# Router columns as weights in four column groups, and the block table built by one-hot products

## Chip, cores and metric

The kernel runs on one core of one Trainium2 chip. The metric is the device time of one execution in microseconds (us). The kernel before takes 2423.96 us, the median of three runs (2423.73 to 2424.24).

## What is computed

One layer of a hybrid backbone over 2048 latent tokens and 256 context tokens of width 1024. Two parallel mixers (an SSD scan with 8 heads, a gated linear attention with 4 heads, both in both directions) share one input and one output projection; then a mixture of experts follows, top 2 of 32 experts, each of inner width 512.

```python
x = x + m_lat[2] * mix_lat
h2_lat = modulate(rmsnorm(x, norm2_g[l]), m_lat[3], m_lat[4])
ffn = moe(h2_lat.reshape(-1, D_MODEL), w_router, router_bias, w_gate[l], w_up[l], w_down[l])
x = x + m_lat[5] * ffn.reshape(x.shape)
...
s = jax.nn.sigmoid((t @ w_router).astype(jnp.float32))          # route(): 2048 x 32 logits
...
dest = pstart[e_sorted] + jnp.arange(T * TOP_K) - start[e_sorted]  # moe(): slot of each choice
buf = jnp.zeros((n_blocks * MOE_BLOCK, D), t.dtype).at[dest].set(t[tok])
yb = lax.map(expert_block, (buf.reshape(n_blocks, MOE_BLOCK, D), block_e))
```

Each of the 4096 choices (2048 tokens, 2 each) gets a slot; a block is 128 slots of one expert. An expert's block needs for each slot the number of its token and its gate. That is the block table.

## The kernel before

It is a row of stages, each a block of per-engine programs that ends with a barrier of all engines: `constants` and `modulation`, `projection`, `chunks`, `mixer`, `slots`, `experts`, `combine`. Within a stage each engine runs its list in the written order, and semaphores tie them.

**mixer** (16 tiles of 128 tokens, 18 steps). In step n, `now` is tile n, `before` tile n-1, `done` tile n-2. TensorE's order in a step is `attn(now)`, `ssd(now)`, `turned_m(before)` (8 transposes), `gla(now)`, `turned_x(done)` (8 transposes), `project(before)` (48 products of 512 columns), `router(done)`. The router's product of a tile is 8 matmuls over the width (L1556): the tile's features `xsT` are the weights, and 32 columns of `w_rt` stream through; the sum stands in 32 columns of the PSUM tile `po`. `gla(now)` waits for `both_done` and `mid_done`, which VectorE signals.

VectorE's order after a projection is `residual(before)` (L1755, x1 = product + x), then, after ScalarE's `squares_x` (L1453) and GpSimd's `rstd` (L1386, L1389), `scaled_x(before)` (L1763), `logits(done)` (L1725), and in the next step `masked_attn` (L1733 twice, L1738) and `state_mid` (L1649). So the lists of both engines meet twice in a step: VectorE's `residual` waits for the last product of `project`, and TensorE's `gla` waits for `state_mid`.

**slots** computes the routing in some 80 VectorE instructions in a chain. The slot numbers come at L2000. GpSimd then writes the block table `slot_tok` into DRAM: it was cleared by one DMA (L1906), and 32 indirect DMAs (L1911), 16 tiles by 2 choices, put a record of 16 words (token, gate) at each slot. VectorE meanwhile computes the plan of the blocks (L2008 to L2027: each block's expert, when to load weights).

**experts**: TensorE first spreads the output gate (L2218), VectorE copies it (L2282), ScalarE and VectorE split the first weights into a high and a low part (L2163, L2289). GpSimd loads the table (L2122), copies the tokens of a block (L2118) and gathers their rows (L2120, `fetch`). TensorE transposes them (`turn`, L2229), ScalarE and VectorE split them (`features`, L2168 and L2295), and the products follow (`wide`, L2236). In the lists of ScalarE and VectorE the splits of the first two weight pieces stand ahead of the features of blocks 0 and 1.

## Time and profile before

| what | value |
|---|---|
| median of three runs | 2423.96 us |
| the profiled execution | 2428.52 us |
| its span | 2426.8 us |
| TensorE busy | 2164.6 us, 89% |
| VectorE busy | 1624.7 us, 67% |
| ScalarE busy | 1137.1 us, 47% |
| GpSimd busy | 529.8 us, 22% |
| mean granted TensorE clock | 0.937 |

How to read it: the span runs from the first to the last instruction, the execution's own time is 1.7 us longer. Busy shares are means over stages with different limits, so what an edit is worth has to be read in its own stage. `mixer` lies at about 902 to 1318 us of the span, `slots` at 1321 to 1401, `experts` at 1404 to 2360, `combine` behind it. TensorE is written PE, its weight load PEld, VectorE DVE, ScalarE ACT, GpSimd POOL.

### The profile page before, as it was taken

To read this page: it belongs to the slowest core of one execution; us is meant where nothing else is said; L and a number is where in the kernel's file an instruction comes from. 1 tells how busy PE (TensorE), PEld (TensorE's weight loads), DVE (VectorE), ACT (ScalarE), POOL (GpSimd) and SP (SyncE) were. 2 spreads that over 40 slices of the span, in tenths; PEclk is the share of its full clock that TensorE was granted. 3 is DMA by queue.
4 is the path that set the end of the run, shared out by engine and by line. 5 is a ranking of instruction groups with operands and counts; after the bars stand their busy time and mean duration, and the time that the engine had idled before them with its cause. 6 is when DMAs were issued, how large, how long until landed. Compare 5 with 4: busy or idle time off the path is not lost. (4 is left out here: it accounts for less than half of the span.)

```text
span 2426.8 us, 36201 instructions
## 1 busy us (share of the span) xinstructions
PE 2164.6 (89%) x11697; PEld 1709.4 (70%) x11697; DVE 1624.7 (67%) x2071; ACT 1137.1 (47%) x1469; POOL 529.8 (22%) x536
## 2 busy tenths in 40 slices
PE   4999999998999987999996059999999999999980
PEld 2777777776777766888885048878788778778760
DVE  1333333433666667777773449999999999999983
ACT  0222222222555533333331047777777777777763
POOL 1000000000000001233322423333332333333332
PEclk7999999999999996899997579999999999999995
DMA  8123334322688745899874426478988779989957
GB/s 317 66 78 108 110 117 145 128 99 85 228 291 295 277 171 191 305 311 293 291 240 113 176 54 207 115 241 275 303 253 274 233 233 356 310 293 309 374 182 293
DMA packets 204877, 530.22 MB, mean 218 GB/s; under 512 B 14929, under 2 KB 46156, under 8 KB 198252
## 3 DMA queue, kind: packets, MB, share of 16 engines
q1 hardware_dynamic: 174904, 424.71, 48.8%
q0 software_dynamic: 26224, 91.57, 15.0%
q10 hardware_dynamic: 3651, 12.65, 1.4%
q8 instruction: 61, 1.00, 0.2%
q14 instruction: 37, 0.30, 0.0%
HBM read 398.64 MB, written 130.24 MB: 218 GB/s over the span
## 5 line engine op out<-in xcount | busy, mean ns | idle before, releaser
L2163 ACT ACTIVATE w_hi_e<-w_gates 128x2048 fp32r (+1 forms) x103 | 197.7, 1920 | 237.1 <-issue 104.1
L2289 DVE TENSOR_TENSOR w_lo_e<-w_gates,w_hi_e 128x2048 fp32r<-128x2048 f32 x103 | 236.4, 2296 | 33.2 <-ACT w_hi_e L2163 33.2
L2289 DVE TENSOR_TENSOR w_lo_e<-w_ups,w_hi_e 128x2048 fp32r<-128x2048 f32 x102 | 233.5, 2289 | 37.0 <-ACT w_hi_e L2163 37.0
L2289 DVE TENSOR_TENSOR w_lo_e<-w_downs,w_hi_e 128x2048 fp32r<-128x2048 f32 x100 | 228.4, 2284 | 0.0
L2163 ACT ACTIVATE w_hi_e<-w_ups 128x2048 fp32r (+1 forms) x102 | 195.2, 1914 | 24.8 <-PE pd_e L2236 22.4
L2163 ACT ACTIVATE w_hi_e<-w_downs 128x2048 fp32r x100 | 191.1, 1911 | 1.0
L614 PE MATMUL pf<-raws,w_in_sb 128*128 128x256 f32 x800 | 177.5, 385 | 1.1 <-DVE raws L695 1.1
L2236 PE MATMUL pg_e<-w_hi_e,x_hi_e 128*128 128x512 f32 x408 | 167.7, 411 | 7.2 <-DVE w_lo_e L2289 7.2
L614 PEld LDWEIGHTS pf<-raws,w_in_sb 128*128 128x128 f32 x800 | 154.1, 193 | 23.0 <-DVE raws L695 1.5
L2141 POOL DMA_INDIRECT x_mid<-yb_e,to_e x50 | 126.9, 2538 | 190.7 <-DVE yb_e L2333 188.6
L2236 PE MATMUL pg_e<-w_lo_e,x_hi_e 128*128 128x512 f32 x408 | 162.1, 397 | 0.0
L2236 PE MATMUL pd_e<-w_hi_e,h_hi_e 128*128 128x512 f32 x400 | 162.1, 405 | 0.0
L2236 PE MATMUL pg_e<-w_hi_e,x_lo_e 128*128 128x512 f32 x408 | 161.9, 397 | 0.0
L2236 PE MATMUL pd_e<-w_hi_e,h_lo_e 128*128 128x512 f32 x400 | 157.9, 395 | 0.0
L2236 PE MATMUL pu_e<-w_hi_e,x_hi_e 128*128 128x512 f32 x400 | 157.9, 395 | 0.0
L2236 PE MATMUL pu_e<-w_hi_e,x_lo_e 128*128 128x512 f32 x400 | 157.9, 395 | 0.0
L2236 PE MATMUL pu_e<-w_lo_e,x_hi_e 128*128 128x512 f32 x400 | 157.9, 395 | 0.0
L2236 PE MATMUL pd_e<-w_lo_e,h_hi_e 128*128 128x512 f32 x400 | 157.9, 395 | 0.0
L614 PE MATMUL pf<-hT,w_in_sb 128*128 128x256 f32 x640 | 143.8, 388 | 0.0
L2118 POOL COPY idx_e<-toks_e 128x1 int32 (+1 forms) x54 | 51.5, 954 | 400.7 <-DMA x_mid<-yb_e,to_e 335.9
L614 PEld LDWEIGHTS pf<-hT,w_in_sb 128*128 128x128 f32 x640 | 124.7, 195 | 17.7
L716 DVE TENSOR_SCALAR fm<-u_raw,cols 128x256 f32<-128x256 f32 x54 | 18.2, 411 | 176.2 <-ACT u_raw L506 176.2
(420 smaller groups left out, 4708.4 us busy)
## 6 DMA issues: line engine op xcount, KB each, us to landing
w_gates<-in_w_gate_dram SPq DMA_DIRECT2D x32, 2048.0 KB, 12.1
w_ups<-in_w_up_dram SPq DMA_DIRECT2D x32, 2048.0 KB
w_downs<-in_w_down_dram SPq DMA_DIRECT2D x32, 2048.0 KB
w_mod_half<-in_w_mod_dram SPq DMA_DIRECT2D x16, 1024.0 KB, 7.0
abc_m<-a_rows SPq DMA_DIRECT2D x16, 1024.0 KB, 4.9
recs<-tok_rec SPq DMA_DIRECT2D x15, 968.0 KB, 7.8
qk_rec<-qk SPq DMA_DIRECT2D x14, 1024.0 KB, 3.9
qk<-qk_rec SPq DMA_DIRECT2D x14, 1024.0 KB
```

What stands on the lines that cost most here:

```text
L614: mm = pe.matmul(pf[n % 2][:, f, :], w[:, k, c0:c0 + P], h[:, k, :], start=(k == 0), stop=(k == KT - 1))
L716: i = dve.tensor_scalar(a, b, wt, cols[:, R_CB + f:R_CB + f + 1], ALU.mult, ALU.add)
L2118: pool.tensor_copy(idx[u][:, :], toks[:, bass.ds(b, 1), 0]).then_inc(idx_ready, 1)
L2141: pool.indirect_dma_start(out=x_mid, out_offset=bass.IndirectOffsetOnAxis(ap=to[u][:, 0:1], axis=0), in_=yb[:, :], in_offset=None, compute ...
L2163: act.activation(w_hi[:, s % 3:s % 3 + 1, :], raw(part, half, place), ACT.Copy).then_inc(hi_done, 1)
L2236: mm = pe.matmul(acc[:, :], a[:, k, :], w[:, s % 3, c], start=start and n == 0, stop=stop and n == 2)
L2289: dve.tensor_tensor(w_lo[:, s % 3:s % 3 + 1, :], raw(part, half, place), w_hi[:, s % 3:s % 3 + 1, :].bitcast(F32), ALU.subtract).then_inc( ...
```

## The change

**In the mixer** the router's product is turned round. The 32 columns of `w_rt` are now the weights and the 128 tokens of `xsT` stream; the matmul of part k goes to column group k % 4 and so to PSUM partitions 32j to 32j+31, so that four sums over two parts each stand under one another. ScalarE copies them (`quartered`), and one step later TensorE adds the four (`logit_sums`, one matmul with the copy as weights and `sum4`, four identities under one another). `logits` on VectorE moves behind `masked_attn` of the next step.

**In slots** the table no longer goes through DRAM. A slot is split into its place in the block and its block. For each of four chunks (choice by half of the tiles) VectorE builds one-hot rows of the place (128 wide) and of the block (68 wide), the latter times the token number and the gate; TensorE multiplies them, 32 matmuls that sum into one PSUM tile, and VectorE copies it to `toks`, which `experts` now reads from SBUF. The clearing DMA, the 32 indirect DMAs and the loading DMA are gone.

```diff
+        sum4, quarters = K["st"][0][:, 0, 0:NE], K["rec"][0][:, D + SW:D + SW + P]
...
             def turned_x(t):
                 if t:
-                    act.wait_ge(log_ps, t)
+                    act.wait_ge(quarter_ps, t)
...
+            def quartered(t):
+                act.wait_ge(quarter_ps, t + 1)
+                if t:
+                    act.wait_ge(log_ps, t)
+                act.activation(quarters[:, :], po[:, 0, 256:256 + P], ACT.Copy).then_inc(quarter_done, 1)
...
+                if done is not None:
+                    quartered(done)
                 if before is not None:
                     squares_x(before)
...
                 for k in range(KT):
-                    mm = pe.matmul(po[:, 0, 256:256 + NE], xsT[:, k, :], w_rt[:, k, :], start=(k == 0), stop=(k == KT - 1))
-                mm.then_inc(log_ps, 1)
+                    j = k % 4
+                    mm = pe.matmul(po[32 * j:32 * j + 32, 0, 256:256 + P], w_rt[:, k, :], xsT[:, k, :], start=(k < 4), stop=(k >= 4))
+                mm.then_inc(quarter_ps, 1)
+
+            def logit_sums(t):
+                pe.wait_ge(quarter_done, t + 1)
+                pe.wait_ge(sum4_done, 1)
+                pe.matmul(po[:, 0, 256 + P:256 + P + NE], quarters[:, :], sum4[:, :], start=True, stop=True).then_inc(log_ps, 1)
...
                     attn(now)
+                if n >= 3:
+                    logit_sums(n - 3)
+                if now is not None:
                     ssd(now)
...
                     router(done)
+            logit_sums(LT - 1)
...
+            dve.tensor_reduce(sum4[:, :], ident[:, :].rearrange("p (j c) -> p c j", j=4), AX, ALU.add).then_inc(sum4_done, 1)
...
                     masked_attn(now)
+                if n >= 3:
+                    logits(n - 3)
+                if now is not None:
                     state_mid(now + CT, now)
...
-                if done is not None:
-                    logits(done)
+            logits(LT - 1)
...
+            for c in range(4):
+                pe.wait_ge(parts_done, c + 1)
+                for i in range(LT // 2):
+                    mm = pe.matmul(table[:, :, :].rearrange("p a b -> p (a b)"), in_place[c % 2][:, i, :],
+                                   parts[c % 2][:, i, :, :].rearrange("p a b -> p (a b)"), start=(c + i == 0), stop=(c == 3 and i == LT // 2 - 1))
+                mm.then_inc(parts_used, 1)
...
-            pool.dma_start(slot_tok.rearrange("(b p) c -> p b c", p=P), zero_i[:, :].rearrange("p (b c) -> p b c", c=16)).then_inc(cleared, 16)
-            pool.wait_ge(cleared, 16)
-            pool.wait_ge(slot_done, 1)
-            for t in range(LT):
-                for j in range(2):
-                    pool.indirect_dma_start(out=slot_tok, out_offset=bass.IndirectOffsetOnAxis(ap=route["slot"][:, t, j:j + 1], axis=0),
-                                            in_=slot_rec[:, t, j, :], in_offset=None).then_inc(scattered, 16)
-            pool.wait_ge(scattered, 16 * 2 * LT)
...
-            then(dve.tensor_copy(slot_rec[:, :, :, 1].bitcast(F32), route["gate"][:, :, :]))
-
...
-            dve.sem_inc(slot_done, 1)
+            then(dve.tensor_scalar(pos_i[:, :, :], route["slot"][:, :, :], P - 1, None, ALU.bitwise_and))
+            then(dve.tensor_copy(pos[:, :, :], pos_i[:, :, :]))
+            then(dve.tensor_tensor(blk_of[:, :, :], slot_f[:, :, :], pos[:, :, :], ALU.subtract))
+            then(dve.tensor_scalar(blk_of[:, :, :], blk_of[:, :, :], 1.0 / P, None, ALU.mult))
+            then(dve.tensor_tensor(val[:, :, :], tok_f[:, :].unsqueeze(2).to_broadcast([P, LT, 2]), pos[:, :, :], ALU.subtract))
+
+            H = LT // 2
+            for c in range(4):
+                j, t, b = c // 2, slice(H * (c % 2), H * (c % 2 + 1)), c % 2
+                if c >= 2:
+                    dve.wait_ge(parts_used, c - 1)
+                dve.tensor_tensor(in_place[b][:, :, :], place[:, :].unsqueeze(1).to_broadcast([P, H, P]),
+                                  pos[:, t, j].unsqueeze(2).to_broadcast([P, H, P]), ALU.is_equal)
+                then(dve.tensor_tensor(in_block[b][:, :, :], bnum[:, :].unsqueeze(1).to_broadcast([P, H, TAB]),
+                                       blk_of[:, t, j].unsqueeze(2).to_broadcast([P, H, TAB]), ALU.is_equal))
+                for n, of in enumerate((val, route["gate"])):
+                    op = dve.tensor_tensor(parts[b][:, :, n, :], in_block[b][:, :, :], of[:, t, j].unsqueeze(2).to_broadcast([P, H, TAB]), ALU.mult)
+                op.then_inc(parts_done, 1)
...
+            dve.wait_ge(parts_used, 4)
+            dve.tensor_tensor(toks[:, :, 0], table[:, 0, :], own[:, :], ALU.add).then_inc(plan_done, 1)
+            dve.tensor_copy(toks[:, :, 1].bitcast(F32), table[:, 1, :]).then_inc(plan_done, 1)
+            dve.wait_ge(plan_done, 2)
...
-            pool.dma_start(toks[:, :, :], slot_tok.rearrange("(b p) c -> p b c", p=P)).then_inc(toks_loaded, 16)
-            pool.wait_ge(toks_loaded, 16)
```

How the lists of the engines change at three places. TensorE in one middle step of the mixer, from the router's product to `gla`, before (lines as in the kernel before):

```order
L1556 MATMUL po_m<-w_rt_m,xsT_m 128x32 x8
L1589 MATMUL at_m<-qk 128x128 x8
L1567 MATMUL py_m<-recs,M_m 128x64 x8
L1575 MATMUL py_m<-st_m,cs_m 128x64 x8
L1575 MATMUL py_m<-st,cs_m 128x64 x8
L1525 MATMUL tr_m<-ident,m_m 128x128 x8
L1607 MATMUL po_m<-recs,both_m 128x128 x2
```

and now (the router's product is L1568, the sum of the quarters L1574, `gla` L1624):

```order
L1568 MATMUL po_m<-xsT_m,w_rt_m 32x128 x8
L1606 MATMUL at_m<-qk 128x128 x8
L1574 MATMUL po_m<-st,recs 128x32
L1584 MATMUL py_m<-recs,M_m 128x64 x8
L1592 MATMUL py_m<-st_m,cs_m 128x64 x8
L1592 MATMUL py_m<-st,cs_m 128x64 x8
L1536 MATMUL tr_m<-ident,m_m 128x128 x8
L1624 MATMUL po_m<-recs,both_m 128x128 x2
```

The eight matmuls of the router give 32 rows of 128 columns instead of 128 rows of 32, and one matmul more stands behind `attn`.

VectorE in the same step, from `residual` to `state_mid`, before:

```order
L1755 TENSOR_TENSOR x_m<-tr_m,x_m 128x512 x2
L1763 SCALAR_TENSOR_TENSOR xs_m<-x_m,rsx_m,scale_bc_m 128x1024
L1725 TENSOR_TENSOR logits<-po_m,rt_shift_m 128x32
L1733 TENSOR_TENSOR am_m<-at_m,incl_bd 128x512 x2
L1738 TENSOR_TENSOR both_m<-am_m 128x512
L1649 SCALAR_TENSOR_TENSOR st_m<-st_m,fc 128x128 x2
```

and now:

```order
L1777 TENSOR_TENSOR x_m<-tr_m,x_m 128x512 x2
L1785 SCALAR_TENSOR_TENSOR xs_m<-x_m,rsx_m,scale_bc_m 128x1024
L1755 TENSOR_TENSOR am_m<-at_m,incl_bd 128x512 x2
L1760 TENSOR_TENSOR both_m<-am_m 128x512
L1747 TENSOR_TENSOR logits<-po_m,rt_shift_m 128x32
L1670 SCALAR_TENSOR_TENSOR st_m<-st_m,fc 128x128 x2
```

`logits` has moved by two places and is still ahead of `state_mid` (L1670 now).

ScalarE at the end of the same step now, where `quartered` is L1441 and `squares_x` L1462 (before, L1453 came straight behind the exponential of `cs_m`):

```order
L1424 ACTIVATE E_m<-E_m 128x512 x2
L1428 ACTIVATE cs_m<-cs_m 128x1024
L1441 ACTIVATE recs<-po_m 128x128
L1462 ACTIVATE recs,ssx_m<-x_m 128x1024
L1513 DMA x_mid<-x_m 128x1024
```

The copy of the quarters stands ahead of `squares_x`.

## Rows read from the trace of the kernel before

**Rows 1.** Stages: span, busy (instructions) of PE, PEld, DVE, ACT, POOL; clock; DMA; GB/s.
```profile
500.00:600.00 100.00, 94.92 (x422) 66.74 (x420) 40.77 (x97) 28.11 (x44) 1.08 (x3) 1.00 0.19 63
...
1020.00:1060.00 40.00, 40.00 (x350) 34.63 (x349) 30.46 (x54) 15.58 (x40) 13.82 (x18) 1.00 0.88 287
...
1320.00:1404.00 84.00, 4.41 (x6) 1.67 (x6) 35.60 (x85) 1.91 (x2) 39.94 (x42) 0.52 0.50 172
...
1600.00:2360.00 760.00, 752.42 (x3450) 605.71 (x3448) 708.21 (x496) 552.14 (x412) 265.75 (x166) 1.00 0.86 283
```
**Rows 2.** Timeline of PE, router to router: start us, duration us, engine, line, instruction, tiles, count.
```profile
1064.45 1.87 PE L1556 MATMUL po_m<-w_rt_m,xsT_m 128*128 128x32 f32 x16
1066.24 1.16 PE L1589 MATMUL at_m<-qk 64*128 64x128 f32 x16
...
1086.70 1.87 PE L1556 MATMUL po_m<-w_rt_m,xsT_m 128*128 128x32 f32 x16
```
**Rows 3.** Timeline of DVE and PEld at the start of `gla`: step 2, then a middle step.
```profile
979.82 0.61 DVE L1649 SCALAR_TENSOR_TENSOR st_m<-st_m,fc 128x128 f32<-128x128 f32 x2
...
980.49 0.93 PEld L1607 LDWEIGHTS po_m<-recs,both_m 128*128 128x128 f32 x4 [1.05 <-DVE both_m L1738]
...
1072.09 0.52 PEld L1607 LDWEIGHTS po_m<-recs,both_m 128*128 128x128 f32 x4
```
**Rows 4.** Timeline of DVE and ACT in that middle step.
```profile
1064.48 1.29 DVE L1755 TENSOR_TENSOR x_m<-tr_m,x_m 128x512 f32<-128x512 f32 x2 [2.33 <-PE tr_m L1545]
...
1065.80 1.06 ACT L1453 ACTIVATE recs<-x_m 128x1024 f32<-128x1024 f32 x1 [6.25 <-DVE x_m L1755]
...
1068.12 1.28 DVE L1763 SCALAR_TENSOR_TENSOR xs_m<-x_m,rsx_m,scale_bc_m 128x1024 f32<-128x1024 f32 x1 [2.35 <-POOL rsx_m L1389]
1069.32 0.18 DVE L1725 TENSOR_TENSOR logits<-po_m,rt_shift_m 128x32 f32<-128x32 f32 x1
1069.42 1.28 DVE L1733 TENSOR_TENSOR am_m<-at_m,incl_bd 128x512 f32<-128x512 f32 x2
...
1071.42 0.61 DVE L1649 SCALAR_TENSOR_TENSOR st_m<-st_m,fc 128x128 f32<-128x128 f32 x2
```
**Rows 5.** Timeline of PEld and PE in the projection: products in column groups of 32.
```profile
90.53 0.16 PEld L267 LDWEIGHTS mod_acc<-w_mod_half,cond_silu 128*32 128x32 f32 x8 [0.33 <-issue]
...
91.42 1.05 PE L628 MATMUL psm<-raws,w_small 128*32 128x256 f32 x16
```
**Rows 6.** Timeline, end of the mixer and `slots`: PE, DVE, ACT and POOL.
```profile
1313.97 3.62 PE L1556 MATMUL po_m<-w_rt_m,xsT_m 128*128 128x32 f32 x16 [0.69 <-ACT xsT_m L1432]
1317.63 0.19 DVE L1725 TENSOR_TENSOR logits<-po_m,rt_shift_m 128x32 f32<-128x32 f32 x1 [6.26 <-PE po_m L1556]
1321.08 1.28 ACT L1877 ACT_TABLE_LOAD   x1 [7.16 <-PEq L107]
...
1355.92 0.18 DVE L2000 CAST slot<-slot_f_r 128x32 int32<-128x32 f32 x1
...
1364.33 0.14 DVE L2027 CAST plan<-eb_r 1x1 int32<-1x1 f32 x1
...
1398.35 0.96 POOL L1911 DMA_INDIRECT slot_tok<-slot_rec_r,slot  x1 [0.30 <-issue]
```
**Rows 7.** Timeline, start of `experts`: PEld, POOL, DVE and PE.
```profile
1404.29 3.49 PEld L2218 LDWEIGHTS pd_e<-ident,mod 128*128 128x128 f32 x16 [53.55 <-issue]
...
1404.83 2.96 POOL L2122 DMA_DIRECT2D toks_e<-slot_tok  x1 [5.52 <-POOLq L107]
...
1411.38 4.49 DVE L2289 TENSOR_TENSOR w_lo_e<-w_gates,w_hi_e 128x2048 fp32r<-128x2048 f32 x2 [1.98 <-ACT w_hi_e L2163]
1414.49 1.43 POOL L2118 COPY idx_e<-toks_e 128x1 int32<-128x1 int32 x1 [6.70 <-DMA toks_e<-slot_tok]
...
1423.83 1.94 PE L2229 MATMUL tx_e<-ident,xg_e 128*128 128x128 f32 x8 [0.65 <-DVE x_lo_e L2295]
...
1425.42 0.78 PE L2236 MATMUL pg_e<-w_hi_e,x_hi_e 128*128 128x512 f32 x1
```

More of the change, by code:

```diff
@@ L198, in build @@
             loaded = [names(f"{n}_loaded") for n in ("gates", "ups", "downs")]
-            slots(nc, A, C, route, slot_tok, weights, loaded, x_mid, h_rows)
-            experts(nc, A, C, route, slot_tok, weights, loaded, h_rows, x_mid)
+            toks = ctx.enter_context(nc.sbuf_tensor("toks", [P, TAB, 2], I32))
+            slots(nc, A, C, route, toks, weights, loaded, x_mid, h_rows)
+            experts(nc, A, C, route, toks, weights, loaded, h_rows, x_mid)
         combine(nc, A, x_mid, out)
@@ L1296, in mixer @@
             sem(n) for n in ("x_added", "x_square", "x_rstd", "x_scaled", "rows_added"))
-        xt_ps, xt_done, log_ps, log_done = (sem(n) for n in ("x_transposed", "xT_done", "logits_product", "logits_done"))
+        xt_ps, xt_done, quarter_ps, quarter_done, log_ps, log_done = (
+            sem(n) for n in ("x_transposed", "xT_done", "logit_quarters", "quarters_copied", "logits_product", "logits_done"))
+        sum4_done = sem("sum_4_done")
         block = ctx.enter_context(nc.Block())
@@ L1724, in logits @@
                 dve.wait_ge(log_ps, t + 1)
-                dve.tensor_tensor(route["logits"][:, t, :], po[:, 0, 256:256 + NE], rt_shift[:, :], ALU.add).then_inc(log_done, 1)
+                dve.tensor_tensor(route["logits"][:, t, :], po[:, 0, 256 + P:256 + P + NE], rt_shift[:, :], ALU.add).then_inc(log_done, 1)
             def masked_attn(t):
@@ L1818, in load_part, with slots @@
                  A[("w_gate", "w_up", "w_down")[n]][0][e].rearrange("(k p) f -> p k f", p=P)).then_inc(w_loaded[n], 16)
-def slots(nc, A, C, route, slot_tok, weights, w_loaded, x_mid, h_rows):
+def slots(nc, A, C, route, toks, weights, w_loaded, x_mid, h_rows):
     logits, plan = route["logits"], route["plan"]
@@ L1852, in slots @@
         last = sb("last", [1, 1])
-        bnum = sb("bnum", [1, TAB])
+        bnum = sb("bnum", [P, TAB])
+        place, own = sb("place", [P, P]), sb("own", [P, TAB])
+        tok_f, val = sb("tok_f", [P, LT]), sb("val", [P, LT, 2])
+        pos_i, pos, blk_of = sb("pos_i", [P, LT, 2], I32), sb("pos", [P, LT, 2]), sb("blk_of", [P, LT, 2])
+        in_place = [sb(f"in_place{b}", [P, LT // 2, P]) for b in range(2)]
+        in_block, parts = [sb(f"in_block{b}", [P, LT // 2, TAB]) for b in range(2)], [sb(f"parts{b}", [P, LT // 2, 2, TAB]) for b in range(2)]
         npf = sb("npf", [1, MAXB // 2])
         slot_f = sb("slot_f", [P, LT, 2])
-        zero_i = sb("zero_i", [P, TAB * 16], I32)
-        slot_rec = sb("slot_rec", [P, LT, 2, 16], I32)
         spare = sb("spare", [P, D])
         excl, tot, pb = ps("excl", [P, LT, NE]), ps("tot", [P, LT, NE]), ps("pb", [P, 512])
-        bias_loaded, made, sig_done, both_done, ranks_ps, lec_done, bend_ps, slot_done, cleared, scattered, chain = (
+        table = ps("table", [P, 2, TAB])
+        bias_loaded, made, sig_done, both_done, ranks_ps, lec_done, bend_ps, parts_done, parts_used, chain = (
             sem(n) for n in ("bias_loaded", "made", "sigmoid_done", "both_done", "ranks_product", "lec_done", "bend_product",
-                             "slots_done", "table_cleared", "scattered", "chain"))
+                             "parts_done", "parts_used", "chain"))
         plan_done, spare_written = sem("plan_done"), sem("spare_written")
@@ L1927, in over_e @@
                 return x.unsqueeze(2).to_broadcast([P, LT, NE])
-            dve.wait_ge(made, 7)
+            dve.wait_ge(made, 8)
             dve.wait_ge(bias_loaded, 16)
@@ L2008, in _ @@
             then(dve.tensor_scalar(last[:, :], bend[0:1, NE - 1:NE], -1.0, None, ALU.add))
-            then(dve.tensor_tensor(blk[:, :], bnum[:, :], last[:, :].to_broadcast([1, TAB]), ALU.min))
+            then(dve.tensor_tensor(blk[:, :], bnum[0:1, :], last[:, :].to_broadcast([1, TAB]), ALU.min))
             then(dve.tensor_tensor(past[:, :, :], by_block(blk[:, :]), by_expert(bend[0:1, :]), ALU.is_ge))
@@ L2027, in _, with experts @@
             then(dve.tensor_copy(plan[:, PL_PAIRS:PL_PAIRS + 1], eb[:, 0:1]))
-            dve.sem_inc(plan_done, 1)
-def experts(nc, A, C, route, slot_tok, parts, w_loaded, h_rows, x_mid):
+            dve.wait_ge(parts_used, 4)
+            dve.tensor_tensor(toks[:, :, 0], table[:, 0, :], own[:, :], ALU.add).then_inc(plan_done, 1)
+            dve.tensor_copy(toks[:, :, 1].bitcast(F32), table[:, 1, :]).then_inc(plan_done, 1)
+            dve.wait_ge(plan_done, 2)
+def experts(nc, A, C, route, toks, parts, w_loaded, h_rows, x_mid):
     mod, ident, plan = C["mod"], C["ident"], route["plan"]
@@ L2130, in _ @@
             pool.wait_ge(gate_done, 2)
-            pool.tensor_copy(to[0][:, :], toks[:, 0, 0:2]).then_inc(to_ready, 1)
+            pool.tensor_copy(to[0][:, :], toks[:, 0, :]).then_inc(to_ready, 1)
             def body(r, u):
```

20 lines of the change are left out of this document (11 added, 9 removed).

## Prediction, written before the result was known

> **What bounds the kernel now.** I first cut the span into stages with the table of windows. In the middle of the mixer PE is busy in all 40.00 of 40 us at full clock, and in the experts in 752.42 of 760; between them lies a stretch of 84 us in which PE does 4.41 us, GpSimd and VectorE have half the time each and the granted clock stands at 0.52 [rows 1]. So there are two questions: is PE's work in the mixer really what sets its time, and what is the chain through `slots` and into the first product of the experts.
>
> For the mixer I read PE's timeline and beside it the other engines'. A step's router takes 1066.24 - 1064.45 = 1.79 us, the next one starts at 1086.70, so a step is 22.25 us [rows 2]; `gla` loads its first weights at 1072.09 [rows 3]. Beside it a chain runs from the last product of `project` over the others: x1 on DVE from 1064.48, the square on ACT from 1065.80, two small ones on POOL, `scaled_x` at 1068.12, `logits`, `masked_attn`, `state_mid` from 1071.42 to 1072.03 [rows 4]. Apart from hand-overs no engine of it pauses. `gla` needs its end. Does it wait for it? In step 2 PE was plainly idle before `gla` (1.05 us): there `state_mid` ended at 979.82 + 0.61 = 980.43 and the first weight load came at 980.49, 0.06 us later. In the middle step the end is 1072.03 and the load 1072.09, again 0.06 [rows 3]. So `gla` is released by VectorE already, and PE's list arrives at the same moment. From `gla` to the end of `project` PE decides, from there to `gla` the chain does: work taken from PE between those two points buys nothing.
>
> For `slots` I read VectorE's and GpSimd's timelines. The slots are known at 1355.92 + 0.18 = 1356.10. DVE ends its plan at 1364.47 and rests; POOL issues 32 indirect DMAs, the last from 1398.35 to 1399.31 [rows 6]. The experts' first instruction comes at 1404.29, then POOL loads the table (1404.83), has it at 1414.49, and the first product of an expert starts at 1425.42 [rows 7]. From the slots to that product it is 69 us with hardly any arithmetic on the path. All of the experts stage is PE's [rows 1], so a shift of its start carries to the end.
>
> **The change, part by part.**
>
> *Mixer, middle steps.* The router is 16 records of 128 x 32 weights with 128 columns streaming. The nearest row has the same weights and 256 columns: 16 records in 1.05 us [rows 5]; half the columns give about 0.5, with 1.05 as the upper end. The sum of quarters is 2 of the old router's 16 records, 1.79 / 8 = 0.22 us. PE so gains 1.79 - 0.5 - 0.22 = 1.07 us between `project` and `gla`. I set this at **0**: the chain covers it, and a wait of PE on VectorE of about 1 us appears before each of the 13 `gla` from step 3 on. On the chain, `logits` (0.10 us from its start to the next, 1069.32 to 1069.42 [rows 4]) only moves, still ahead of `state_mid`. ScalarE gets a copy of 128 x 128 ahead of the square. It must end before 1065.80, that is 1.35 us after the router's start. With 0.5 us of router, some 0.2 of result latency (1.87 busy against 1.79 to the next [rows 2] is 0.08, taken double) and a third of a us for the copy, it ends at about 1.1 and is hidden; the cover is 0.25 us. The ends of the range: -0.5 us a step if the router takes 1.05, and +1.07 if my reading of the release is wrong.
>
> The weight load at a change from whole to 32-column weights stood idle 0.33 us before it [rows 5]. The Trainium skill, "TensorEngine Tiling (Array Packing)", Key Properties, says that a change of tiling mode drains the TensorE, which speaks against putting such products between whole ones. By that rule the router ends 0.33 us later, the copy misses its cover by 0.08 us, and the sum would be 1.1 us (14 squares) less. I keep 0, since the 0.33 may be hidden in part behind running products.
>
> *Mixer, both ends.* `sum4` is one DVE reduction of 128 x 128 ahead of the first copies, 0.3 us lost. The last tile: today from the router (1313.97, half clock) to `logits` (1317.63) 3.66 us [rows 6]. Now the router at half clock takes 1.0 (twice 0.5), with latency 1.2, the copy 0.4, the sum at half clock twice 0.22 with latency 0.6: 2.2. That is 1.4 less, but the last DMA into `h_rows` also ends about there, so I take 1.0 (0 to 1.4). Mixer in all: **0.7 gained**.
>
> *Slots.* Five small VectorE instructions come in before the rounds and one goes, at 0.22 each (0.18 and a hand-over): +0.9, so the rounds start at 1357.0. A round has 1024 elements a partition for the place and three times 544 for the block. 1024 took 1.20 us from start to next start (1068.12 to 1069.32), two times 512 1.28 [rows 4]: 1.2 + 0.75 (it waits for its own end) + 2 x 0.64 = 3.2 us, four rounds 12.8. PE's products: per round 16 records of 128 x 136. At half clock 16 records of 128 columns take 3.49 us of weight loads [rows 7], so 3.7 with 136. That is slower than DVE, which from round 3 on has to wait for a buffer: 0.4 us, so 13.2 in all, to 1370.2. The last product ends near 1357.0 + 3.2 + 4 x 3.7 = 1375.0; behind that hide the plan's instructions, which take 1364.47 - 1356.10 = 8.4 us as before, but now behind the rounds: 1378.6. Two copies of 68 columns from PSUM, 0.5: 1379.1. The barrier: from the end of `logits` 1317.82 to 1321.08, 3.26 us [rows 6]. The experts start at 1382.3 instead of 1404.29: **22.0 gained**. Bounds: 19 (4 rounds at 4 us) to 23.5 (no waits, 3 us a round). POOL's instructions fall away; what is left on it is long done.
>
> *Start of the experts.* Without the load POOL copies the tokens 0.54 us after PE's start instead of 1414.49 - 1404.29 = 10.2, so the gather of block 1 would be ready 9.66 us earlier, at +9.9 from the start. What is late next: DVE splits two weight pieces until 1411.38 + 4.49 = 1415.87, +11.6, and only then the features of block 0. The second turn needs the first of these (+12.2), and the first product follows it by 1425.42 - 1423.83 = 1.6 us [rows 7]: +13.9 instead of +21.1. **7.2 gained**; bounds 6 and 9.7.
>
> Sum: 0.7 + 22.0 + 7.2 = 29.9 us. The profiled execution took 2428.52 us with a span of 2426.8; its span should become 2396.9. Against the median of the runs, which lies 4.6 us lower than that execution, the same 29.9 gives 2423.96 - 29.9 = **2394.0 us**.
>
> **The rivals.**
>
> *A: PE sets the mixer.* For it: 40.00 of 40.00 busy [rows 1]. Against it: the two equal distances of 0.06 us [rows 3]. Then 13 steps give 1.07 more each, 13.9: 2380.
>
> *B: the copy delays the square.* If the four column groups run one after another, the router takes its old 1.87, the copy ends at 1.87 + 0.35 = 2.2 and the square comes 0.85 us late in 14 steps: 12 us back, 2406. For it: the copy's cover is 0.25 us. Against it: 16 records of double size in 1.05 us [rows 5].
>
> *C: the one-hot rounds cost twice* (two broadcast operands, half of them with a stride): 13 us more, 2407. Against it: `masked_attn` too has a broadcast operand and takes 0.6 us for 512 [rows 4].
>
> *D: slower than before, by the clock.* The new waits of 1 us in each step of 22 could bring the granted clock down from 1.00, that is from 2.4 to 1.2 GHz. The 48 products of a projection fill most of the 1086.70 - 1072.09 = 14.6 us between `gla` and the next router [rows 2, 3]; I estimate that at the lower level 11 us of it are added. In all 13 steps that is 143 us, so 2394 + 143 = 2537; the change is slower from the point where one step in five loses its clock (30 / 143). Against it: between 500 and 600 us PE was busy 94.92 of 100 us, pausing for as large a share as it will now (1 in 22), at a clock of 1.00 [rows 1]. The Trainium skill, "TensorE: Matmul & The Clock Gate", section A second HAM failure mode, tells of a kernel in which frequent short pauses between groups of matmuls made the clock swing between its two levels. By that rule this rival would come true; the trace so far disagrees.
>
> **Numbers.** My forecast 0.80 (2388 to 2400 by the bounds of the parts), A 0.06, B 0.07, C 0.04, D 0.03. The range, 2386 to 2402, takes in the forecast's own spread with some of the half-way forms of A and B and leaves their full forms, C and D out. A measurement of this kernel can tell about 0.2%, 4.8 us, from no change. Faster by more than that: all but D and some unknown trouble, 0.96; within it 0.01; slower 0.03.
>
> **What would show it.** In the changed kernel's profile: `gla`'s first load 0.06 us behind the end of `state_mid` and a PE wait of about 1 us on VectorE in each of 13 steps, the steps still 22.3 us apart; the router's 16 records in about 0.5 us; the square still 1.35 us behind the router's start; four rounds in 13 us; 3.3 us of barrier; the first product of an expert 13.9 us behind the experts' first instruction; 752 of 760 us busy PE in the experts as before. The prediction is wrong if the steps are shorter than 22.0 us (A), if `squares_x` waits for the copy (B), if a round takes over 4 us (C), or if the clock in the mixer is under 0.98 (D).

## The result and the profile after

The changed kernel takes **2393.82 us** (median of 4 runs, 2392.3 to 2395.27) against 2423.85 us before in the same session, a ratio of 0.9878 with a 95% interval of 0.9861 to 0.9895, that is 25 to 34 us less. Forecast were 2394.0 us and a range of 2386 to 2402. The profiled execution took 2392.3 us and has a span of 2390.5 us. All comparisons here and below take runs of the fast state alone; one of the twelve executions of the kernel with nine sums (2619.66 us at a mean granted clock of 0.81) and one of the kernel before beside it (4088.01 us at 0.78) were slow and are left out.

The table of windows, as in [rows 1]; the columns are stretch, length, busy time and instructions of PE, PEld, DVE, ACT and POOL, clock, DMA share, GB/s:

```profile
1060.00:1260.00 200.00, 193.24 (x1674) 159.90 (x1673) 147.00 (x252) 72.57 (x189) 62.28 (x81) 1.00 0.86 289
1318.00:1376.00 58.00, 14.94 (x70) 11.60 (x70) 48.90 (x107) 1.06 (x2) 2.09 (x4) 0.62 0.64 236
```

In the middle of the mixer PE was busy in 40 of 40 us and now rests 6.8 of 200 us, 0.75 us in each step of 22.27, at an unchanged clock. The stretch that holds `slots` is down from 84 to 58 us, and VectorE fills most of it.

A middle step, PE's timeline, to be held against [rows 2]; the next router is at 1083.17, so a step is 22.27 us, and before it was 22.25:

```profile
1060.90 0.64 PE L1568 MATMUL po_m<-xsT_m,w_rt_m 128*32 128x128 f32 x16
1061.48 1.16 PE L1606 MATMUL at_m<-qk 64*128 64x128 f32 x16
1062.57 0.41 PE L1574 MATMUL po_m<-st,recs 128*128 128x32 f32 x2
```

The other engines in that step, against [rows 3, 4]:

```profile
1060.85 1.29 DVE L1777 TENSOR_TENSOR x_m<-tr_m,x_m 128x512 f32<-128x512 f32 x2 [2.33 <-PE tr_m L1556]
1061.61 0.28 ACT L1441 ACTIVATE recs<-po_m 128x128 f32<-128x128 f32 x1 [5.68 <-PE po_m L1568]
1062.17 1.06 ACT L1462 ACTIVATE recs<-x_m 128x1024 f32<-128x1024 f32 x1 [0.28 <-DVE x_m L1777]
...
1067.79 0.60 DVE L1670 SCALAR_TENSOR_TENSOR st_m<-st_m,fc 128x128 f32<-128x128 f32 x2
...
1068.46 0.52 PEld L1624 LDWEIGHTS po_m<-recs,both_m 128*128 128x128 f32 x4 [0.96 <-DVE both_m L1760]
1068.50 0.68 PE L1624 MATMUL po_m<-recs,both_m 128*128 128x128 f32 x4 [0.75 <-DVE st_m L1670]
```

The router takes 0.58 us instead of 1.79 (from its start to the next product's) and the sum 0.24. Its 16 records start in fours, 0.007 us apart within a group (1060.902, .908, .915, .922) and a group every 0.11 to 0.13 us, where the old router started one record every 0.11 us: the four column groups run side by side. The square waits for x1 and not for the copy. `state_mid` ends at 1068.39, the first weight load of `gla` comes 0.07 us later, and most of what used to be work of PE is now its wait (0.75 us on PE, 0.96 on its weight load).

The end of the mixer, against [rows 6]:

```profile
1307.95 0.93 POOL L1413 DMA_DIRECT2D h_rows<-xs_m  x1 [1.73 <-DVE xs_m L1785]
1310.36 1.08 PE L1568 MATMUL po_m<-xsT_m,w_rt_m 128*32 128x128 f32 x16 [0.69 <-ACT xsT_m L1435]
...
1312.51 0.19 DVE L1747 TENSOR_TENSOR logits<-po_m,rt_shift_m 128x32 f32<-128x32 f32 x1 [4.76 <-PE po_m L1574]
1317.15 1.28 ACT L1905 ACT_TABLE_LOAD   x1 [5.37 <-PEq L107]
```

From router to `logits` it is 2.15 us instead of 3.66, but from the end of `logits` to the first instruction of `slots` 4.45 instead of 3.26. What stands there is on GpSimd: it waits for its last DMA into `h_rows` to land and then for its own DRAIN, which closes its list for the stage. Time to landing and DRAIN before, then the DRAIN in the changed kernel (POOLq is GpSimd's sequencer; durations in ns, start in us):

```profile
DMA to landing us min/median/max: 5.6/5.6/5.6
...
L1243 POOLq DRAIN  x1: 2666/2666/2666, 1317.3 to 1317.3; - x1
...
L1243 POOLq DRAIN  x1: 2666/2666/2666, 1313.4 to 1313.4; - x1
```

Before, the DMA landed at 1317.15 and the DRAIN ended at 1320.00; now it lands at 1313.21 and the DRAIN ends at 1316.06. From its end to the first instruction of `slots` it is 1.08 and 1.09 us.

`slots` from the known slots on, VectorE's timeline, then PE's over the same time:

```profile
1352.08 0.18 DVE L2028 CAST slot<-slot_f_r 128x32 int32<-128x32 f32 x1
...
1353.40 1.22 DVE L2040 TENSOR_TENSOR in_place_r<-place_r,pos_r 128x1024 f32<-128x1024 f32 x1
...
1360.74 1.23 DVE L2040 TENSOR_TENSOR in_place_r<-place_r,pos_r 128x1024 f32<-128x1024 f32 x1 [0.92 <-PE table_r L1918]
...
1367.08 0.13 DVE L2053 TENSOR_SCALAR last_r<-bend_r 1x1 f32<-1x1 f32 x1
...
1367.50 2.41 DVE L2055 TENSOR_TENSOR past_r<-blk_r,bend_r 1x2176 f32<-1x2176 f32 x1
1369.95 2.41 DVE L2056 TENSOR_REDUCE eb_r<-past_r 1x68 f32<-1x2176 f32 x1
...
1375.06 0.22 DVE L2075 COPY toks<-table_r 128x68 f32<-128x68 f32 x1
```

```profile
1356.71 6.29 PE L1918 MATMUL table_r<-parts_r,in_place_r 128*128 128x136 f32 x32 [9.67 <-DVE parts_r L2045]
1364.05 2.12 PE L1918 MATMUL table_r<-parts_r,in_place_r 128*128 128x136 f32 x16 [1.05 <-DVE parts_r L2045]
1367.22 2.12 PE L1918 MATMUL table_r<-parts_r,in_place_r 128*128 128x136 f32 x16 [1.05 <-DVE parts_r L2045]
```

The start of the experts, against [rows 7]:

```profile
1376.26 3.49 PEld L2263 LDWEIGHTS pd_e<-ident,mod 128*128 128x128 f32 x16 [7.12 <-issue]
...
1376.36 0.18 POOL L2165 COPY idx_e<-toks 128x1 int32<-128x1 int32 x1 [55.96 <-POOLq L107]
...
1390.18 0.78 PE L2281 MATMUL pg_e<-w_hi_e,x_hi_e 128*128 128x512 f32 x1
```

From the cast of the slots to the experts' first instruction it was 1404.29 - 1355.92 = 48.37 us and is 1376.26 - 1352.08 = 24.18. From there to the first product it was 21.13 and is 13.92. These two, 24.2 and 7.2 us, are nearly all of the change. The two profiles differ by 36.3 us, since the stages ahead of the mixer, which the change leaves alone, came out 3.0 us shorter in the second one (VectorE's first instruction of `mixer` at 894.41 against 897.41) and others by a microsecond here and there. The medians are the better measure of the whole, the rows of the parts.

### The profile page after: what moved, and what is told of

It is laid out like the page before. It is cut to its first block and busy times, and to the rows that moved or that the text cites. A ratio compares the mean times of both kernels' runs of the same rounds, so it can differ in the third digit from the quotient of the medians.

```text
span 2390.5 us, 36428 instructions
## 1 busy us (share of the span) xinstructions
PE 2158.2 (90%) x11793; PEld 1692.7 (71%) x11793; DVE 1638.0 (69%) x2094; ACT 1140.7 (48%) x1485; POOL 497.3 (21%) x503
## 5 line engine op out<-in xcount | busy, mean ns | idle before, releaser
L2208 ACT ACTIVATE w_hi_e<-w_ups 128x2048 fp32r (+1 forms) x102 | 195.7, 1919 | 23.7 <-PE pd_e L2281 22.5
L2165 POOL COPY idx_e<-toks 128x1 int32 (+1 forms) x54 | 53.2, 985 | 447.4 <-DMA x_mid<-yb_e,to_e 333.7
```

Of the source, the lines that this page charges most:

```text
L2165: pool.tensor_copy(idx[u][:, :], toks[:, bass.ds(b, 1), 0]).then_inc(idx_ready, 1)
L2208: act.activation(w_hi[:, s % 3:s % 3 + 1, :], raw(part, half, place), ACT.Copy).then_inc(hi_done, 1)
```

## The experiments

Each is a whole kernel, timed beside the one before. "The whole change" below is the changed kernel, 2393.82 us. A step is the distance from one router to the next in PE's timeline; in each kernel all middle steps but the ones named agree within 0.03 us.

### Half the change each

`e1_router_only` takes the mixer of the changed kernel and the `slots` and `experts` of the one before, `e2_table_only` the reverse.

> Only the mixer's half of the change: column-group router, copy, sum and the moved logits, with the table of slots still made by 32 indirect DMAs and loaded by the experts. My theory (a mixer step is set by the chain over the other engines, so the microsecond that PE saves turns into a wait for state_mid): steps of 22.3 us as before, only the mixer's ends gain, so 0.4 to 1 us less than the kernel before, about 2423. Rival A (PE sets the step): 13 steps of 1.07 us, 14 us less, about 2410. Rival B (the copy delays the square): up to 12 us more, about 2436.

> Only the other half: the table by one-hot products and kept in SBUF, with the old router. My theory: all of the gain is here, about 29 us less than the kernel before, 2394 to 2396, that is within 1 us of the whole change. Rival A gives 2408 (14 us of the gain would be the router's), rival B 2382 (the router would have cost 12 us of it).

Measured: router only **2423.61** (ratio 1.0002, 0.9993 to 1.0011), table only **2393.01** (0.9881, 0.9865 to 0.9896). The steps are 22.26 and 22.27 us. All of the gain is the table's, within what the runs can tell. By the interval of the router-only kernel, its part is worth between 2.7 us lost and 1.7 gained. Rival A and the full form of B are out.

### Is VectorE's chain what the step waits for?

Both kernels move one VectorE operation, the masked attention, out of the chain, on the new router (`e3_masked_early`) and on the old one (`e4_old_router_masked_early`):

```
+                if n == 0:
+                    masked_attn(0)
                 if now is not None:
-                    masked_attn(now)
...
                     residual(before)
+                if more:
+                    masked_attn(now + 1)
+                if before is not None:
                     scaled_x(before)
```

> The whole change, and on VectorE the masked attention of the next tile moved from between logits and state_mid to ahead of scaled_x of this step, behind the x1 residual, where VectorE waits for the square and its root. It takes about 1.3 us out of the chain that ends in state_mid and leaves PE's list alone. My theory: PE's wait of 0.8 to 1.1 us for state_mid before each of 13 gla goes, each step shortens from 22.27 to about 21.3 us, 11 to 13 us less than the whole change, about 2382. Rival (PE has hidden waits elsewhere in the stretch, such as the copies of the turned x, that take its place): less than 4 us, about 2391. If scaled_x is delayed by the moved work instead, the transposes of the step come later and it may be slower.

> The same reordering on VectorE on the kernel with the table only (old router of 1.79 us on PE). My theory: chain and PE's list arrive at gla at the same time there, so that once the chain is shorter PE's own list still fills the whole step, 22.2 us: no more than 2 us less than the table only, about 2394. Together with the other three kernels: neither the lighter router alone nor the shorter chain alone gives anything, both together 11 to 13 us. Rival (the chain alone sets the step, PE has slack there): the same 11 to 13 us as with the new router, about 2383.

| | masked attention as it was | early |
|---|---|---|
| old router | 2393.01, step 22.27 | 2387.4, step 22.19 |
| new router | 2393.82, step 22.27 | 2381.78, step 21.29 |

PE's timeline of `e3_masked_early`: nothing stands in brackets any more, `gla` follows the transposes at once.

```profile
1065.78 1.09 PE L1536 MATMUL tr_m<-ident,m_m 128*128 128x128 f32 x8
1066.70 0.61 PE L1624 MATMUL po_m<-recs,both_m 128*128 128x128 f32 x4
```

The early kernels stand at 0.9852 (0.9837 to 0.9867) with the old router and 0.9821 (0.9807 to 0.9834) with the new one. With the chain out of the way the router is worth 22.19 - 21.29 = 0.90 us a step. Alone neither edit moves a step by 0.1 us, together they take 0.98. `e3` gains 12.0 us on the whole change, where 11 to 13 were expected. `e4` gains 5.6 us in the median where at most 2 were expected, so that expectation missed by 3.6. 13 steps of 0.08 us are 1.0 of it; in its profile the first router comes 81.59 us behind the first product of the mixer's setup against 83.66 in `e2`, so 2.1 us more fall in the first steps, where PE stood waiting before [rows 3], and the last two steps are 0.2 us shorter. Together that is about the 3.1 us between the two profiled executions (2391.15 and 2388.04); they are the fastest of `e2` and the slowest of `e4`, and the other 2.5 us of the medians are not shown by any trace.

### How much room has the copy?

`e5_copies` issues three more copies of the quarters on ScalarE, into unused columns, ahead of the real one:

```
+                for i in range(3):
+                    if t or i == 2:
+                        act.wait_ge(spared, 3 * t + max(i - 1, 0))
+                    act.activation(spare[:, i % 2, :], po[:, 0, 256:256 + P], ACT.Copy).then_inc(spared, 1)
                 act.activation(quarters[:, :], po[:, 0, 256:256 + P], ACT.Copy).then_inc(quarter_done, 1)
```

> The whole change with three more copies of the router's 128 x 128 quarters on ScalarE, ahead of the one that counts, in each of 14 steps: by the copy's row of 0.28 us that is 0.8 to 0.9 us more before the square, of which a cover of 0.28 us hides a part. Rival B's mechanism (the square and all behind it slides by what exceeds the cover): 0.5 to 0.6 us a step, 7 to 8 us more than the whole change, about 2401. If ScalarE has more slack than the one row shows: no change, 2394. If the copy had no cover at all already: 12 us more, 2406.

Measured: 2397.96 (0.9891, 0.9876 to 0.9906), 4 us more, and steps of **22.37**, 0.10 us more, 1.4 us in 14 steps. The expectation, 7 to 8 us more, was too high. The rest of the 4 us can't be laid to the copies: in its profile the stages ahead of the mixer, which have no such copy, are 5.7 us longer than in the changed kernel's. The timeline of ScalarE:

```profile
1066.61 0.61 ACT L1446 ACTIVATE recs<-po_m 128x128 f32<-128x128 f32 x3 [5.69 <-PE po_m L1574]
1067.10 0.30 ACT L1447 ACTIVATE recs<-po_m 128x128 f32<-128x128 f32 x1
...
1067.26 1.08 ACT L1468 ACTIVATE recs<-x_m 128x1024 f32<-128x1024 f32 x1
```

I took 0.28 us, the busy time of a copy, for its price. In a row they come every 0.16 us, and the square follows the last start by 0.16 too. Three copies cost 0.49, the room is 1062.17 - 1061.61 - 0.16 = 0.40, and the remaining 0.09 is what the square came late (1.36 us behind the router's start instead of 1.27) and what the step grew. So the mechanism of rival B is real and starts at 0.4 us; the change stays below.

### How much room has PE, and what does the clock do?

Two kernels issue the sum of quarters nine times and five times:

```
-                pe.matmul(po[:, 0, 256 + P:256 + P + NE], quarters[:, :], sum4[:, :], start=True, stop=True).then_inc(log_ps, 1)
+                for _ in range(9):
+                    mm = pe.matmul(po[:, 0, 256 + P:256 + P + NE], quarters[:, :], sum4[:, :], start=True, stop=True)
+                mm.then_inc(log_ps, 1)
```

> The whole change with the product that sums the quarters issued nine times instead of once: 8 x 0.24 = 1.95 us more on PE between project and gla, in 13 steps (and once behind the last). My theory (PE waits 0.8 to 1.1 us there for state_mid): the wait takes half of it, so 0.95 us a step shows, 12 to 14 us more than the whole change, about 2407. If PE set the step already: 25 us more, 2419. If the wait were longer than I read: under 6 us, 2400.

> The whole change with the sum of the quarters issued five times. Nine times gave 18 records in 2.03 us, so four more cost PE 0.90 us a step; the run with nine lengthened the step by 0.81 where 1.79 was added, so PE's wait is 0.97 us. My theory: 0.90 fits into the wait, steps stay at 22.27 us and the time is that of the whole change, 2394. The clock: with nine sums it fell to half in 3 of 13 steps and cost 3.2 us each time. If it falls whenever PE has no pause left, it falls here too, about 10 us more, 2403; but the kernel before had no pause either and no fall, so I expect none.

Nine sums: **2416.36** (0.9979, 0.9967 to 0.9991), 22.5 us more than the whole change, nine more than the 2407 expected. 18 records take 2.03 us, so 1.79 were added, and the step grew by 0.81: the room on PE is 0.98 us, as read. But three of the 13 steps took 26.25 us instead of 23.08. The windows of three neighbouring steps:

```profile
1018.40:1041.48 23.08, 23.08 (x203) 19.57 (x202) 16.42 (x29) 8.06 (x21) 6.92 (x9) 1.00 0.88 293
1041.48:1067.72 26.24, 26.24 (x203) 22.64 (x202) 16.52 (x29) 8.18 (x21) 6.91 (x9) 0.87 0.78 257
1067.72:1090.80 23.08, 23.08 (x203) 19.57 (x202) 16.42 (x29) 8.06 (x21) 6.90 (x9) 1.00 0.86 282
...
1047.00:1053.00 6.00, 6.00 (x44) 5.76 (x44) 3.18 (x10) 0.60 (x1) 1.17 (x2) 0.50 0.84 186
```

For 6.8 us PE ran at 1.2 instead of 2.4 GHz, though it had not paused once; the fall began at 1046.6, 1.5 us behind the start of the last of the nine sums. The long steps are the 3rd, the 7th and the 11th of the 13. This profile is of the quickest of the executions, 2411.86 us; how often the clock fell in the others, which go up to 2427.55, isn't known.

Five sums: steps of 22.27 as expected, the added 0.90 us vanish in the wait. No fall of the clock was expected, but one step took 25.32 us with a clock of 0.87, and the six runs lie at 2391.64 to 2405.76, median **2397.99** (0.9898, 0.9878 to 0.9918). The two fastest, 2391.64 and 2392.02, equal the whole change; that they had no fall is likely, but only one execution (2395.42) was traced.

That is the loss of rival D, but met by adding work where D had it from pauses. `e11_chain_pad` goes the other way, PE's list as it is and the chain longer (the two mask products of VectorE issued twice):

```
-                for hh in range(2):
+                for n, hh in enumerate((0, 1, 0, 1)):
                     dve.wait_ge(at_ps, t + 1)
+                    if n >= 2:
+                        dve.wait_ge(am_done, 4 * t + n - 1)
```

> The whole change with the two mask products of VectorE issued twice, which lengthens the chain to state_mid by two instructions of 0.64 us, 1.3 us, and leaves PE's list alone: PE's pause before gla grows from 1.0 to 2.3 us in each of 13 steps. If the chain sets the step: 23.55 us instead of 22.27, 14 x 1.3 = 17 to 18 us more than the whole change, about 2411 with the clock at 1.00 all through. Rival D of the prediction (pauses of PE bring the clock down): clock under 1.00 in the mixer's steps and 3.2 us more for every step in which it falls, as in the run with nine sums; three such steps give 2421, all thirteen 2453. If only a PE that never pauses is slowed, there is no fall here.

`e12_filled` is the same, with eight wide products in the pause:

```
+                if now is not None and n >= 3:
+                    for k in range(8):
+                        pe.matmul(po[:, 1, 256:512], w_hi[:, k, 0:P], w_hi[:, k, 0:256], start=True, stop=True)
                 if now is not None:
                     gla(now)
```

> The run with the lengthened chain, and in PE's pause of 1.9 us before gla eight products of 128 x 128 weights with 256 columns, whose results are written to an unused part of a bank and never read; they are extra work and leave nothing out. If they take up to 1.9 us the chain still sets the steps. In the run without them the clock fell in 7 of 13 steps and cost 14.6 us in its profile, in the run with nine sums in 3 of 13, though PE never paused there. Theory S (the clock falls when this stretch holds too little streaming, pauses and small products alike): with the pause filled by wide products it stays at 1.00, steps of 23.46 us, 13 to 15 us less than the run without them, about 2412. Theory P (it falls after pauses, and in the run with nine sums by something else): the pause is gone here too, so it gives the same 2412, but then the nine sums should not have fallen. Theory C (some extra load or power sets it, whatever PE does in the pause): falls as often or more often, 2428 or over.

Measured: longer chain **2428.02** (1.0014, 1.0004 to 1.0025), filled **2410.76** (0.9944, 0.9931 to 0.9958). With the longer chain the clean steps are 23.46 us (1.2 more, PE's pause 1.94 instead of 0.75), three take 26.3 to 26.4 and five 24.9 to 25.0, so that the clock cost 3 x 2.9 + 5 x 1.5 = 16.2 us in 8 of 13 steps. The chain alone was to give 2411; the rest came as the expectation's rival D had it, in more steps than the three it named. (The expectation for the filled kernel says 7 steps and 14.6 us; one of the middle ones was overlooked in it.) The windows of a clean step, one of the long and one of the middle ones, and the fall itself:

```profile
1045.75:1069.21 23.46, 21.53 (x187) 17.82 (x186) 17.50 (x31) 8.06 (x21) 6.91 (x9) 1.00 0.85 281
1069.21:1095.61 26.40, 24.46 (x188) 20.20 (x187) 17.52 (x31) 8.06 (x21) 6.90 (x9) 0.87 0.86 300
1095.61:1120.55 24.94, 23.00 (x188) 18.85 (x187) 17.53 (x31) 8.06 (x21) 6.92 (x9) 0.93 0.72 241
...
1077.00:1084.00 7.00, 6.00 (x48) 4.93 (x49) 6.93 (x16) 1.87 (x10) 1.35 (x2) 0.55 0.93 279
```

Filled, all 13 steps take 23.45 to 23.47 us, at the same length of chain and a clock of 1.00:

```profile
1075.17 1.09 PE L1536 MATMUL tr_m<-ident,m_m 128*128 128x128 f32 x8
1076.01 1.20 PE L1648 MATMUL po_m<-w_hi_m 128*128 128x256 f32 x8
1078.20 0.68 PE L1624 MATMUL po_m<-recs,both_m 128*128 128x128 f32 x4 [0.99 <-DVE st_m L1673]
```

Extra work of no use made the kernel 17 us faster. But the last row also shows that the pause was not gone, as the expectation had it: it fell from 1.94 to 0.99 us, near the 0.75 of the whole change, where the clock didn't fall either. So this run can't tell whether the wide products took the falls away or the shorter pause alone did; a run that shortens the pause without adding products is missing. What is shown: the falls come with a pause of 1.94 us, and with no pause when more products of 32 columns are issued; they stay away with pauses of 0.75 and 0.99 us. A theory of pauses alone (P) can't explain the nine sums, and C is spoken against by the filled kernel. S fits all of it and remains a reading, not shown. Why only some of the 13 steps are hit, these runs don't tell.

### Can the rest be had?

`e7_plan` works out the expert of each block with the blocks on partitions, ahead of the rounds, and turns the column by one product:

```
+            then(dve.tensor_scalar(last_c[:, :], bend[:, NE - 1:NE], -1.0, None, ALU.add))
+            then(dve.tensor_tensor(last_c[:, :], bcol[:, :], last_c[:, :], ALU.min))
+            then(dve.tensor_tensor(past_c[:, :], last_c[:, :].to_broadcast([P, NE]), bend[:, :], ALU.is_ge))
+            dve.tensor_reduce(eb_c[:, :], past_c[:, :], AX, ALU.add).then_inc(ebc_done, 1)
...
+            pe.matmul(pb[:, NE:NE + TAB], eb_c[:, :].to_broadcast([P, P]), C["ident"][:, 0:TAB], start=True, stop=True).then_inc(eb_ps, 1)
...
-            then(dve.tensor_tensor(past[:, :, :], by_block(blk[:, :]), by_expert(bend[0:1, :]), ALU.is_ge))
-            then(dve.tensor_reduce(eb[:, :], past[:, :, :], AX, ALU.add))
+            then(dve.tensor_copy(eb[:, :], pb[0:1, NE:NE + TAB]))
```

> The whole change, and the plan's expert of each block worked out with the blocks on partitions (four small VectorE instructions ahead of the rounds and one small product behind them, with a copy of 68 columns from PSUM) instead of two instructions of 2176 elements on one partition, 2.41 us each. My theory: behind the rounds the plan is the path to the experts' start (toks come last), so 4.8 us go and about 0.8 come back: 3.5 to 4.5 us less than the whole change, about 2390. The product for it stands behind PE's table products, which end near the same time; if these hold it: 2 to 3 us less. Rival (the start of the experts waits for something else, such as DMAs of weights): no change, 2394.

> The whole change with both edits: masked attention of the next tile early on VectorE, and the plan with the blocks on partitions. They lie in different stages, so if both theories hold the gains add: 15 to 17 us less than the whole change, about 2378. If the reordering gives nothing, about 2390.

Plan: **2387.81** (0.9858, 0.9844 to 0.9873), 6.0 us less than the whole change, where 3.5 to 4.5 were expected. From the slots' cast to the end of `toks` VectorE takes 18.14 us instead of 23.20, and 0.71 ahead of the cast for the four small ones: 4.35 less, as reckoned. The other 1.7 stand at the start of the experts:

```profile
1372.80 0.22 DVE L2075 COPY toks<-table_r 128x68 f32<-128x68 f32 x1
1374.02 1.86 PEld L2263 LDWEIGHTS pd_e<-ident,mod 128*128 128x128 f32 x16 [2.08 <-issue]
1374.05 2.02 PE L2263 MATMUL pd_e<-ident,mod 128*128 128x128 f32 x16 [1.91 <-PEq L107]
```

In the changed kernel PE rests 7 us between the last product of the table and this first work of the experts, and does it at half clock, 3.49 us of weight loads. Now it rests 2 us and does it in 1.86. Both edits: **2374.54** (0.9801, 0.9788 to 0.9814), 19.3 less than the whole change, where 15 to 17 were expected; 12.0 and 6.0 were measured alone, so the two gains add within what the runs can tell.

`e9_start` adds a reordering at the start of the experts, alike on ScalarE and VectorE:

```
-                if s == 1:
-                    features(0, 0)
-                    features(1, 1)
+                if s < 2:
+                    features(s, s)
```

> Both edits of the run before (masked attention early, plan with the blocks on partitions), and at the start of the experts the features of block 0 split right behind the first piece of weights on ScalarE and VectorE, those of block 1 behind the second, instead of both behind the second. In the profile of the run with both edits the first product of an expert starts at 1371.42, 2.3 us behind the end of the second weight split; the features of block 0 now come one split (2.2 us) earlier. My theory: the first product 1.9 to 2.2 us earlier and all behind it too, about 2372.5. Rival: the second half of the first expert's weights, which is now split later on VectorE by the features' 1.3 us, holds the second group of products and takes it back: no change, 2374.5.

Measured: **2370.76** (0.9783, 0.977 to 0.9795), 3.8 less than without it in the medians. The first product starts at 1369.17, 9.99 us behind the experts' first instruction at 1359.18; before this edit it was 1371.42 - 1359.23 = 12.19. So 2.2 us are the edit's, as expected; the other 1.6 of the medians are not shown by a row. This kernel beats the one before by 53 us (2423.31 in its session) and the changed one by 23.

## Why the prediction was right

The sum was 29.9 us and the medians give 30.0. The mechanism held in the middle steps of the mixer, in the rounds of the table and at the start of the experts; at the two ends of stages, the mixer's and that of `slots`, it did not. The closeness is partly luck, since the terms were off to both sides, and the parts as measured, 0.4 + 24.2 + 7.2 = 31.8 us (31.5 less the 0.3 reckoned for `sum4`), are themselves more than the medians give:

| term | reckoned | measured |
|---|---|---|
| mixer, middle steps | 0 | 0 (steps 22.27 and 22.25) |
| router and sum on PE | 0.5 and 0.22 | 0.58 and 0.24 |
| mixer's last tile | 1.0 | 0.4 |
| rounds of the table | 13.2 | 13.68 |
| plan behind the rounds | 8.4 | 7.8 |
| barrier to the experts | 3.26 | 0.98 |
| slots to experts' start, gained | 22.0 | 24.2 |
| start of the experts, gained | 7.2 | 7.2 |

*Middle steps.* The reading that paid was 0.06 us between the end of `state_mid` and `gla`'s first load, in a stage where PE was busy in 40.00 of 40 us [rows 1, 3]. A busy engine that arrives at the same moment as its last operand has no waits to show, and yet a lighter list on it gains nothing by itself. The two-by-two table above shows both halves of it.

*The copy.* Hidden, as forecast, with 0.4 us of room rather than 0.25. On the change of tiling mode: the waits view of the changed kernel shows a pause of PE's weight load ahead of the router in every step.

```profile
PEld po_m L1568 <- issue: 3.7, 10, 0.4
```

That is 0.37 us each. The Trainium skill, "TensorEngine Tiling (Array Packing)", Key Properties, has such a drain, and the trace agrees that something of that size stands there; but the price put on it, 1.1 us for the kernel, did not come. The 0.37 lie for the most part beside products that are still running: the router's first product starts 0.32 us behind the last one of `project`, where products follow each other there every 0.24, so that PE's list loses 0.08 us a step, and the copy keeps its room. With it PE saves 1.79 - 0.58 - 0.24 - 0.08 = 0.89 us a step, which is what the two kernels with the chain out of the way gave (0.90).

*Mixer's end.* Here the step "I take 1.0 (0 to 1.4)" was too high. From PE's last router to `logits` 1.5 us went, as reckoned (1.4), but from the router before the last to the start of `slots` it is 14.38 us after 14.79, only 0.4 less. The end is set by the DMA into `h_rows`: from its issue to the first instruction of `slots` it is 1321.08 - 1311.57 = 9.51 us in the profile before, 1317.15 - 1307.95 = 9.20 after, and 1319.05 - 1309.69 = 9.36 with the router alone, whatever `logits` does. These are 5.6, 5.3 and 5.4 us to its landing, then in all three 2.67 us of GpSimd's DRAIN and some 1.1 of barrier.

*Barrier.* The term "The barrier: from the end of `logits` 1317.82 to 1321.08, 3.26 us" failed by the same rows. What I had measured was for the most part GpSimd's DRAIN, which ran until 1320.00 behind a DMA that had landed 0.67 us before `logits` ended, and then 1.08 us of barrier. `slots` had such an end too: behind the last indirect DMA GpSimd's DRAIN took 2.92 us, until 1403.55, and it went with the indirect DMAs. Where GpSimd has long been done, from the end of `toks` at 1375.28 to the experts at 1376.26, the barrier is 0.98 us, and in the eleven experiments that have this table 0.97 to 1.00. That is 2.3 us of gain not reckoned; the rounds took back 0.5.

*Rounds.* VectorE waited 0.92 us for PE before the third round instead of 0.4, because PE's first two rounds, 32 records in 6.29 us, ran at half clock until 1361.5; then the clock came up and the 16 of a round took 2.12. That VectorE sets the rounds with 3.2 us each was right, and rival C is out.

*Rival D.* It didn't come true in this change: 193.24 of 200 us busy at a clock of 1.00, no long step. But 0.03 was too little for how near it lies: lengthening PE's pause from 0.75 to 1.94 us is enough to lose 16.2 us to the clock, in 8 of 13 steps. And its price was far too high. The estimate of 11 us a step took the whole of `project` at the lower level; the falls met here lasted at most 6.8 us and cost 1.5 to 3.2 us each, so that the 2537 us of all 13 steps would have been some 2436 (2394 + 13 x 3.2, an estimate). The Trainium skill, "TensorE: Matmul & The Clock Gate", section A second HAM failure mode, tells of a clock that swings when the engine idles often between groups of products. With the pauses of the change itself the trace disagrees, with longer ones it agrees, and the kernel with nine sums shows a fall without any pause.

## What to carry over

Before costing a lighter engine list, look at the distance between the end of the last operand and the start of what needs it. If it is the bare hand-over, two chains arrive together and both have to be shortened: 0.98 us a step for the pair here, nothing for either.

A small scatter through DRAM and back (32 indirect DMAs, one every 1.3 us, a DRAIN of 2.9 and a load of 10 us) can be worth replacing by comparisons and products that look wasteful: 32 products and 16 wide VectorE operations took 13.7 us.

The price of a barrier has to be read where nothing else is open. Where GpSimd's list ends with a DMA, one reads the DMA's landing and GpSimd's DRAIN: 9.2 to 9.5 us from issue to the next stage here, against 0.98 for the barrier alone.

## What the runs showed of the hardware

- TensorE's clock can fall to 1.2 GHz for 6.8 us in the middle of a stage in which it never pauses, at 3.0 to 3.2 us a time, once PE's small products of 32 columns are made more (`e6_pad8`, `e10_pad4`). Eight useless products of 256 columns in a pause of 1.94 us, of which 0.99 were left, took the falls away, 2410.76 against 2428.02 us.
- Products in four column groups run side by side: 16 records of 128 x 32 weights with 128 columns took 0.58 us, where 16 records of 128 x 128 weights with 32 columns took 1.79. The change of tiling before them cost PE's list 0.08 us.
- At the end of a stage whose last GpSimd instruction is a DMA with its wait, GpSimd's DRAIN takes 2.67 us ahead of the barrier (all profiles at the end of `mixer`), and 2.92 behind the indirect DMAs of the kernel before; where GpSimd had long been done it took 0.21 and held nothing up.
- After TensorE was idle for 7 us the next 16 products ran at 1.2 GHz (3.49 us of weight loads); after 2 us they ran at 2.4 GHz and took 1.86.
- Copies of 128 x 128 from PSUM on ScalarE last 0.28 us each and follow each other every 0.16 us. For work in a row the second number is the price.
